# Attention steps that take both heads of a span, with the queries' remainders on separate row halves of TensorE

## The reference, cut to what matters

```
def stick_breaking(q, k, v, q_pos, k_pos, bias):
    z = einsum('bqhd,bkhd->bhqk', q, k) * d ** -0.5 + bias        # per head
    log_keep  = where(k_pos < q_pos, log_sigmoid(-z), 0)
    tail_excl = reverse exclusive cumsum of log_keep over the keys
    w   = where(k_pos < q_pos, exp(log_sigmoid(z) + tail_excl), 0)
    out = einsum('bhqk,bkhd->bqhd', w, v)
```

## Time and profile before

| | |
|---|---|
| times, 3 runs | 1828.01, 1828.97, 1830.21 us (median 1828.97) |
| the profiled execution | 1828.6 us, of which its span in the profile 1827.0 us |
| mean granted TensorE clock | 0.989 |
| PE (TensorE matmul) busy | 1771.4 us, 97% |
| PEld (TensorE weight load) busy | 1391.7 us, 76% |
| DVE (VectorE) | 966.8 us, 53% |
| ACT (ScalarE) | 775.1 us, 42% |
| POOL (GpSimd) | 266.5 us, 15% |

### The profile page before, as it was taken

How to read it: one execution, slowest core, us unless ns; L and a number is a source line. 1 busy time by engine, 2 the same in 40 slices (tenths; PEclk the granted TensorE clock), 3 DMA queues, 4 the chain that set the end, 5 groups by cost and what they waited for, 6 DMA issues and landing times. The chain is left out here.

```text
span 1827.0 us, 27331 instructions
## 1 busy us (share of the span) xinstructions
PE 1771.4 (97%) x9783; PEld 1391.7 (76%) x9783; DVE 966.8 (53%) x1836; ACT 775.1 (42%) x1651; POOL 266.5 (15%) x324
## 2 busy tenths in 40 slices
PE   5899999999999999999999999999999998999998
PEld 2678787878787878777788877788877776677677
DVE  4554444444444444453545545576615667777652
ACT  3752323232323232332334433343326777888620
POOL 2000000000000000000000022101113545555300
PEclk8899999999999999999999999999999999999999
DMA  9222222222222222366424578424355558795252
GB/s 334 87 76 79 74 81 77 77 77 77 77 77 78 76 77 76 122 217 190 131 77 126 196 221 272 144 75 142 101 159 127 128 127 238 193 241 188 85 170 98
DMA packets 153688, 240.59 MB, mean 132 GB/s; under 512 B 13208, under 2 KB 102096, under 8 KB 152561
## 3 DMA queue, kind: packets, MB, share of 16 engines
q1 hardware_dynamic: 136570, 179.69, 33.3%
q0 software_dynamic: 17024, 59.66, 9.2%
HBM read 177.91 MB, written 61.42 MB: 131 GB/s over the span
## 5 line engine op out<-in xcount | busy, mean ns | idle before, releaser
L479 PE MATMUL rt_acc<-rt_w_hi,rt_h_hi 128*128 128x512 f32 x504 | 203.3, 403 | 1.0 <-DVE rt_h_lo L1021 1.0
L481 PE MATMUL rt_acc<-rt_w_hi,rt_h_lo 128*128 128x512 f32 x504 | 197.2, 391 | 0.0
L480 PE MATMUL rt_acc<-rt_w_lo,rt_h_hi 128*128 128x512 f32 x504 | 196.5, 390 | 0.0
L1700 POOL TENSOR_TENSOR pa_take<-pa_take,pa_after_key 128x512 f32<-128x512 f32 (+2 forms) x152 | 152.8, 1008 | 139.5 <-DVE pa_after_key L2024 134.0
L1064 DVE TENSOR_TENSOR rt_by_cos<-rt_raw,rt_cos 128x256 f32<-128x256 f32 (+1 forms) x72 | 30.5, 424 | 243.8 <-ACT rt_raw L894 243.8
L905 ACT COPY rt_qk_t<-rt_tr 128x256 f32<-128x256 f32 (+1 forms) x72 | 26.0, 361 | 278.6 <-PE rt_tr L713 278.6
L2966 PE MATMUL kq_acc<-kq_w_hi,kq_h 128*128 128x512 f32 x320 | 128.6, 402 | 0.0
L2969 PE MATMUL kq_acc<-kq_w_hi,kq_h 128*128 128x512 f32 x320 | 125.1, 391 | 0.0
L2967 PE MATMUL kq_acc<-kq_w_lo,kq_h 128*128 128x512 f32 x320 | 124.8, 390 | 0.0
L1912 ACT ACTIVATE pa_keep<-z,pa_bias 128x128 f32<-128x128 f32 (+3 forms) x192 | 110.8, 599 | 3.1 <-PE z L1764 2.8
L1912 ACT ACTIVATE pa_take<-z,pa_bias 128x128 f32<-128x128 f32 (+3 forms) x192 | 110.8, 602 | 0.0
(11 more groups left out here) (405 smaller groups left out, 4028.5 us busy)
## 6 DMA issues: line engine op xcount, KB each, us to landing
ro_a_raw<-retained SPq DMA_DIRECT2D x14, 1024.0 KB, 5.9
op_ada<-in_ada_w SPq DMA_DIRECT2D x8, 1024.0 KB, 13.2
rt_w_raw<-in_ret_w_in SPq DMA_DIRECT2D x16, 512.0 KB, 5.1
rt_w_raw<-in_ret_w_in SPq DMA_DIRECT2D x8, 1024.0 KB, 7.6
rt_old<-in_state_ret SPq DMA_DIRECT2D x8, 1024.0 KB, 5.8
rt_g_raw<-in_ret_w_in SPq DMA_DIRECT2D x8, 1024.0 KB, 5.3
out_st_sample<-rt_new POOLq DMA_DIRECT2D x8, 1024.0 KB, 7.8
k_cols<-kq_parts POOLq DMA_DIRECT2D x16, 512.0 KB, 3.9
```

The costliest lines, as they stand in the source:

```text
L479: nc.tensor.matmul(dst, h_hi[:, k, cols], w_hi[:, k, :], start=k == 0, stop=False)
L480: nc.tensor.matmul(dst, h_hi[:, k, cols], w_lo[:, k, :], start=False, stop=False)
L481: last = nc.tensor.matmul(dst, h_lo[:, k, cols], w_hi[:, k, :], start=False, stop=k == KD - 1)
L1700: nc.gpsimd.tensor_tensor(own, own, later, ALU.mult).then_inc(weighed, 1)
```

## The change

The list is now of `groups`: a group is a span, with its one or two pieces, or a sample piece. All engines step by groups.

- Scoring: `score(g)` scores both heads of a span. Head 0 always goes to bank 0 of `z` and head 1 to bank 1. For each head the matmul of `q_hi` runs over all 128 rows; then the two matmuls of `q_lo` run on 64 rows each, head 0 on rows 0 to 63 and head 1 on rows 64 to 127, against the high part of the keys alone. So that this works the keys of head 1 are stacked the other way round and `q_lo` is stored once (heads side by side), which takes 9 DMAs for a pair instead of 12.
- Waits: the `q_hi` matmul of a head waits until the last stick that read that head's bank is done (`bank_freed`).
- Order on TensorE: score g+1, project (two slices in four of five groups), first piece of `turn_w` of group g-1, sample transposes, attend g-2, fold, second piece of `turn_w`. LAG is 1 group, `take` has 6 buffers, `keep` 4.
- Copies of turned weights: VectorE takes the first piece of each group (96), ScalarE the second (64) and the sample pieces (8). Before, VectorE had every third.
- Sample pieces come every 5 groups.

```diff
+            own, to = slice((part ^ hh) * DH, (part ^ hh) * DH + DH), slice(part * DH, (part + 1) * DH)
+            sp.dma_start(k_t[own, hh, :].bitcast(F32), ps.k_cols[half, part * HB + block, dims, :]).then_inc(signal, 16)
             sp.dma_start(q_hi[to, hh, :].bitcast(F32), ps.q_cols[half, block, dims, :]).then_inc(signal, 16)
-            sp.dma_start(q_lo[to, hh, :].bitcast(F32), ps.q_cols[half, HB + block, dims, :]).then_inc(signal, 16)
+    sp.dma_start(q_lo[:].bitcast(F32), ps.q_cols[half, HB + block]).then_inc(signal, 16)
...
-        LAG, TR, WR, KR = 3, 5, 4, 3
+        LAG, TR, WR, KR = 1, 6, 4, 4
...
-        START, FIRST_SLOT, PERIOD, FILL = KD, 3, 24, 19
+        START, FIRST_SLOT, PERIOD, FILL = KD, 3, 5, 4
...
+        def banks_of(p):
+            return pieces[p].heads if pieces[p].b is None else (0,)
+        def bank_freed(p, n):
+            return max([q + 1 for q in range(p) if n in banks_of(q)], default=0)
...
         def on_vector(p):
-            return at.b is None and p % 3 == 0
+            return pieces[p].b is None and p == members[group_of[p]][0]
...
-                for i, hh in enumerate(at.heads):
-                    dst, keys = z[:, p % 2, i * n:(i + 1) * n], k_t[pair % 2][:, hh, c0:c0 + n]
-                    nc.tensor.matmul(dst, q_hi[pair % 2][:, hh, queries], keys, start=True, stop=False)
-                    last = nc.tensor.matmul(dst, q_lo[pair % 2][:, hh, queries], keys, start=False, stop=True)
-                last.then_inc(scored, 1)
+                for hh in range(2):
+                    freed = bank_freed(members[g][0], hh)
+                    if freed:
+                        pe.wait_ge(sticks, freed)
+                    nc.tensor.matmul(z[:, hh, 0:n], q_hi[pair % 2][:, hh, queries], k_t[pair % 2][:, hh, keys], start=True, stop=False)
+                for hh in range(2):
+                    own = slice(hh * DH, (hh + 1) * DH)
+                    last = nc.tensor.matmul(z[:, hh, 0:n], q_lo[pair % 2][own, queries], k_t[pair % 2][own, hh, keys],
+                                            start=False, stop=True, tile_position=(hh * DH, 0))
+                    if hh or len(groups[g]) == 2:
+                        last.then_inc(scored, 1)
...
+            for g in range(NG + LAG + 1):
+                weights = members_at(g - LAG)
+                if g + 1 < NG:
+                    score(g + 1)
+                if g < NG:
+                    project(slices_before(g), slices_before(g + 1))
+                for p in weights[:1]:
+                    turn_w(p)
+                if g in new_slots:
+                    turn_new(new_slots[g])
+                if g in page_slots:
+                    turn_pages(*page_slots[g])
+                if g >= LAG + 1:
+                    attend(g - LAG - 1)
+                if sample_before(g, LAG + 3) is not None:
+                    fold(sample_before(g, LAG + 3))
+                for p in weights[1:]:
+                    turn_w(p)
```

More of the change, by code:

```diff
@@ L1388, in attention @@
             for n, (c0, cols) in enumerate(spans):
[L1389 to L1392, removed]
+                groups.append([Piece(u, heads, c0, cols, n == 0, n == len(spans) - 1)
+                               for heads in ([(0, 1)] if cols <= NB // 2 else [(0,), (1,)])])
+        HALF = len(groups) // 2
+        HP, NK, GR, GW, RING = sa.HP, sa.NK, sa.GR, sa.GW, sa.RING
+        sample_at = [HALF + 9 + 5 * b for b in range(DB)]
         for b in range(DB):
[L1394 to L1397, removed]
+            groups.insert(sample_at[b], [Piece(None, (), 0, NK, False, False, b)])
+        NG = len(groups)
+        pieces = [at for group in groups for at in group]
         NPC = len(pieces)
[L1399 to L1410, removed]
+        members = [[p for p in range(NPC) if pieces[p] in group] for group in groups]
+        group_of = [g for g in range(NG) for p in members[g]]
+        begins = [min(g for g in range(NG) if groups[g][0].u == u) for u in range(UNITS)]
+        ends = [max(g for g in range(NG) if groups[g][0].u == u) for u in range(UNITS)]
+        def banks_of(p):
+            return pieces[p].heads if pieces[p].b is None else (0,)
+        def bank_freed(p, n):
+            return max([q + 1 for q in range(p) if n in banks_of(q)], default=0)
         def scans_done(p):
@@ L1634, in _ @@
             load_g(1)
[L1635 to L1642, removed]
+            v_slots = {ends[NPT * pair - 1] + LAG + 2: pair + 1 for pair in range(1, PAIRS - 1)}
+            g_slots = {ends[NPT * pair - 1] + LAG + 5: pair + 1 for pair in range(1, PAIRS - 1)}
+            turned_at = {max(g for g in page_slots if page_slots[g][0] == b) + 1: b for b in range(DB)}
+            for g in range(NG):
+                u = groups[g][0].u
+                if g in turned_at and turned_at[g] + RING < DB:
+                    load_keys(turned_at[g] + RING)
+                if g == G_END + 1:
                     sp.wait_ge(made, NT)
                     load_samples()
[L1645 to L1651, removed]
+                if u is not None and g == begins[u] and u % NPT == 0 and 0 < u // NPT < PAIRS - 1:
+                    load_pair(u // NPT + 1)
+                if g in v_slots:
+                    load_v(v_slots[g])
+                if g in g_slots:
+                    load_g(g_slots[g])
+                if g == HALF + 5:
                     for n in range(2):
@@ L1783, in attend @@
                     return
[L1784 to L1787, removed]
                 pair, t = where(at.u)
@@ L1854, in _ @@
             project(0, START)
[L1855 to L1869, removed]
-                    turn_gates()
[L1871 to L1876, removed]
+            for g in range(NG + LAG + 1):
[16 more added lines that the diff above has]
+                    turn_w(p)
+                if g == G_END + 3:
+                    turn_gates()
             pe.wait_ge(next_loaded, 16)
@@ L2083, in gate, with gate_at @@
                     dve.sem_inc(gated, 1)
-            def gate_at(p):
-                if pieces[p].u is not None and p == ends[pieces[p].u] and pieces[p].u % 4 == 3:
-                    gate(pieces[p].u)
+            def gate_at(g):
+                if not 0 <= g < NG:
+                    return
+                u = groups[g][0].u
+                if u is not None and g == ends[u] and u % 4 == 3:
+                    gate(u)
             def finish_gates(t):
```

167 lines of the change are left out of this document (79 added, 88 removed).

## The result

The changed kernel takes 1863.06 us (median of 4 runs, 1859.72 to 1863.61), the kernel before 1829.59 in the same comparison: ratio 1.018, 95% interval 1.0168 to 1.0193. It is slower by 33 us, inside the range, 13 us under the forecast of 1876.

The account below looks back on a forecast made before the run. TensorE, working in its fixed order, was taken to bound both halves of the attention stage. First half +17 and second half +30 gave +47 us on 1828.6, so 1876 us, with its own range 1855 to 1895.

Parts of the forecast that it names:

- Part 1: TensorE's scoring: one pass saved per span, two tile-shape changes added; +19 us taken, -23 as lower end.
- the pair itself: The two row-half `q_lo` matmuls of a 512 span: 0.53 us, or 0.68 with the changes of shape.
- Part 2: Score handshake with ScalarE: both banks belong to one group, so TensorE and ScalarE wait; 38.8 us a pair against 28.8.
- A + S: Least time of a group: its sigmoids (2.6 us at 512) plus the score behind them (1.02 us at 512).
- the samples' 43 us of TensorE work: Second half: sample work partly fits into the waits; 10 us was let go there and 33 kept.
- 20 or more: Sign of being right: PE's waits on `z` for ACT's `pa_take` go from 3.7 us to this.
- the clock falls: Rival, chance 0.12: waits in the second half cost TensorE its 2.4 GHz at times; 20 us more, 1896 us.
- Halves: Attention's first half +17 us (+9.4 shapes, +8 waits); second half, pairs 4 to 7 and samples, +30 us.
- +15 if all 24 are used and no gaps are added: Low case of the second half's +30: samples' work fills all 24 us of waits, no gaps counted.
- What hides: Costs put at nothing: the shorter lag, VectorE's 43 further copies (26 us if uncovered), SyncE's queue, the stage's ends.
- faster: Rival, chance 0.13: TensorE stays the bound throughout and the saved pass counts in full; -23 us, 1806 us.
- Cheap shapes: Rival, chance 0.14: row halves overlap fully, shape changes cost nothing, the handshake stays; +9 us, 1838 us.

Follow-up runs that it names:

- e11: e6 with the score banks of the kernel before (bank p % 2, both heads of a narrow span in one bank): 1824.93 us, ratio 0.9978.
- e1: The changed kernel with smaller rings, `take` at 5 and `keep` at 3 buffers, as a control: 1862.81 us, ratio 1.0187.
- e9: The kernel before with the samples' first transposes three pieces later and the sample pieces one piece later: 1822.40 us, ratio 0.9969.
- e2: e1 with both `q_lo` matmuls on all 128 rows again, in the same order: 1849.34 us, ratio 1.0112.
- e4: The kernel before with each of its 192 `q_lo` matmuls on rows 0 to 63 alone, nothing side by side: 1880.82 us, ratio 1.0284.
- e3: e2 with each head's `q_hi` and `q_lo` matmuls together, head 0 before head 1: 1841.98 us, ratio 1.0068.
- e5: The changed kernel with the samples' first transposes three groups later and the sample pieces two groups later: 1852.95 us, ratio 1.0133.
- e10: e6 with copies of turned weights shared as before (VectorE every third piece, ScalarE the others): 1833.23 us, ratio 1.003.
- e7: e1 with a third bank for scores in rotation and the scans' constant operand moved to SBUF: 1886.89 us, ratio 1.032.
- e8: e7 with the samples later, by the shifts of e5: 1876.47 us, ratio 1.0263.
- e6: e3 with the samples later, by the shifts of e5: 1828.07 us, ratio 1.0002.

## Why the prediction was right or wrong

The steps from the changed kernel down to e11 add up. From e1, each a difference of medians: row halves 13.5 us, order of the two heads 7.4, samples' place 13.9 (10 beside the row halves), a bank for each head 3.1. Together 37.9, which leads from 1862.8 to 1824.9. That is 3 us under the kernel before, but not by the group order: with its samples later too, the kernel before takes 1822.4 (e9), 2.5 us less than e11 beside it.

- **Part 1, shapes: right in mechanism, too large.** +19 was put down, and e2 against e1 shows 13.5. (The two aren't quite alike: the +19 already has off it the 0.10 that scoring both heads together saves, which e2 keeps; by the sum's own terms e2 should have gained 0.68 - 0.46 = 0.22 at 512, so the overestimate is larger than it looks.) The mis-sized term is the pair itself: 0.53 us in the sum, 0.44 in the trace at 512. I had the second weight load cost its 0.11 step; the two matmuls take 0.50 together. Here the Trainium skill (TensorE: Matmul & The Clock Gate, Part 3) was right, that the second tile adds next to nothing, and the trace agrees (two in 0.50, one in 0.51 on the mean). The Trainium skill's rule on draining (TensorEngine Tiling, "Key Properties") decided the sign. The trace agrees with that too: 20.5 us of held-up weight loads at `q_lo` here, +52.5 us in e4. The lone price was forecast at 0.3 us and measured at 0.27.
- **Part 2, handshake: right in mechanism, some two to three times too large.** The part of it that stands outside part 1 was 47 - 19 = 28 us: +8 in the first half and about +20 of the second half's +30. The runs give 7.4 for the order of the heads and 3.1 for a bank each, 10 or 11 in all. The step that failed is the second half's sum: I set A + S, which ScalarE needs, as the floor of each group and let the samples' 43 us of TensorE work fill only 10 of the waits. TensorE's own waits for `take` rose by 8.8 us (3.7 to 12.5) on PE, and "20 or more" had been named as the sign; had the floor held, they would have been near 30. ScalarE did wait 53.5 us for scores, as foretold, but e3 has 28.1 of these with little loss: idle time of ScalarE had been read as lost time.
- **What stood in for it: the samples' place, not foreseen.** About 10 to 14 us. The prediction moved the sample pieces in TensorE's order but never followed SyncE's queue to their loads: issued 3 us before TensorE wanted them instead of 10.5. What held them is the load of pair 4's gates, which the new order put ahead of them in the queue; the sum had put SyncE's queue at nothing. The time that this took was named as a rival (the clock falls), but placed in the handshake; the longest stretch, 1560 to 1583 us, came behind a single long wait. That the median lands within 13 us of the forecast owes something to this: the two parts of the sum were about 23 us too large (19 + 28 against 13.5 + 10.5), and this place added 10 that were in no term. That is luck.
- **Halves.** Forecast +17 and +30, measured +6 and +27. The good fit of the second is luck: the wait for the samples' loads and the slow clock behind it lie in the first half of the kernel before and in the second half of the changed one. Two kernels without that wait show it: e5 against e9 has 183 against 169 us and 190 against 171, so +14 and +18. Nor do the row halves cost the same in both, as the sum had it (9.4 each): e1 against e2 has 185.5 against 173.6 and 195.9 against 193.9, so 12 us and 2. In the first half a share of that, up to 7 us, is the clock at its start: some 14 us at the 1.2 GHz level that e2 doesn't have. Why the second half lost so little to the row halves is open.
- **Slips in the sum.** "+15 if all 24 are used and no gaps are added" is 155 + 19 + 8 - 172 = +10. The mark of 1546 us for the second half lies 2 us early: the earlier trace rows has 98 matmuls of `q_hi`, four pairs have 96, and pair 4 begins at 1548.3. Neither moves the forecast.
- **What hides.** The rings cost nothing (e1). The lag leaves 1.3 us of waits for POOL on PE; its price by itself was not measured. The copies were put at nothing; e10 shows that they gain 5 us.
- **The rival "faster"** needed the saved pass to count in full. It didn't: e2 against e1 has the row halves as a loss, and even without the samples' wait shapes and handshake together stand 25 us above before (e5). "Cheap shapes" is refuted by e4 and by e2.

What stays open: the handshake's price with the row halves in place, since e7 and e8 changed VectorE too; and what the changed kernel would gain if only the gates' load went back behind the samples' loads.

## What to carry to other kernels

Count the changes of shape before splitting a matmul onto half of the array's rows: one pair between full-size operations saved a pass of 0.23 us and lost more to two changes of shape. Whether several pairs in a row would pay, no run tested. When the order on the busiest engine is rewritten, follow every load that the order uses from its issue to its first reader, and look at what stands ahead of it in its queue: a wait of 6.6 us there cost twice over, because the clock fell behind it. And an engine that waits is not yet a loss: only the waits of the engine that sets the time are, which a price has to be checked against.

## What the runs showed of the hardware

- A scan whose second operand lies in SBUF is slow only while GpSimd works. A 512-column scan takes 1.27 us alone with the operand in PSUM (e1) or in SBUF (e7). With a GpSimd multiply beside it, it takes 1.28 us in e1 and 1.96 on the mean in e7, while the multiply keeps its 1.09 us in both. The Trainium skill (GPSIMD Engine Reference, "Specifications") says that GpSimd shares SBUF interfaces with VectorE instructions that have two SBUF inputs, and these runs agree.
- After a wait of 6.6 us the granted clock was 0.50 for all of 1560 to 1580 us, though TensorE was busy again from 1565 on; in e6, without that wait, it was 1.00. After waits of 1.67, 0.53 and 0.15 us it was 0.50 from 1385 to 1395.
- Two matmuls on separate row halves take as long as one: on 64 rows 0.50 us at 512 columns and 0.44 to the next operation, and a single one in e4 0.50 and 0.43.
